# A two-layer block on one Trainium2 core: three of the twelve weight subtractions of each expert go from VectorE to GpSimd

## The reference, cut to what matters

```python
def expert_block(args):
    xb, eb = args                       # rows sent to one of 32 experts
    up = jnp.dot(xb, w_up[eb]) + b_up[eb]            # 1024 -> 2048
    glu, lin = jnp.split(up, 2, axis=-1)
    glu = jnp.minimum(glu, SWIGLU_LIMIT)
    lin = jnp.clip(lin, -SWIGLU_LIMIT, SWIGLU_LIMIT)
    act = glu * jax.nn.sigmoid(SWIGLU_ALPHA * glu) * (lin + 1.0)
    return jnp.dot(act, w_down[eb]) + b_down[eb]     # 1024 -> 1024
```

## Time and profile before

| | us |
|---|---|
| median of 3 runs (lowest and highest) | 2296.3 (2295.66 and 2297.38) |
| the profiled execution, its own time | 2296.3 |
| its span, first to last instruction | 2294.5 |
| PE busy over the span | 2163.4 (94%) |
| DVE busy | 1483.6 (65%) |
| ACT busy | 1200.2 (52%) |
| POOL busy | 74.8 (3%) |

### The profile page before, as it was taken

One profiled execution on the slowest core, in us unless ns is written; L12 is line 12 of the kernel. 1 busy time (PEld: TensorE's weight loads), 2 busy tenths in 40 slices (PEclk: granted clock), 3 DMA queues, 4 the chain that ended last, 5 costly groups with the idle time before them and its releaser, 6 DMA issues. The chain is left out here.

```text
span 2294.5 us, 29210 instructions
## 1 busy us (share of the span) xinstructions
PE 2163.4 (94%) x10208; PEld 1688.1 (74%) x10208; DVE 1483.6 (65%) x1509; ACT 1200.2 (52%) x1252; POOL 74.8 (3%) x51
## 2 busy tenths in 40 slices
PE   7899996899999999999999999999996889799988
PEld 4675345688888888888888888888884478667777
DVE  1303303789999899899898999989995145234401
ACT  1111402677776777777777777777773126522210
POOL 0000000000000000000000000000000013311000
PEclk8998997799999999999999999999998999899999
DMA  9753602598888888888988898898894433223420
GB/s 329 194 177 131 231 13 92 173 307 307 303 302 310 307 308 298 305 305 303 313 304 300 306 304 306 306 305 300 305 315 170 156 126 123 98 74 110 143 78 19
DMA packets 252653, 525.24 MB, mean 229 GB/s; under 512 B 27442, under 2 KB 34714, under 8 KB 252474
## 3 DMA queue, kind: packets, MB, share of 16 engines
q1 hardware_dynamic: 240538, 521.40, 65.8%
q10 hardware_dynamic: 12064, 3.15, 0.9%
HBM read 522.88 MB, written 1.06 MB: 228 GB/s over the span
## 5 line engine op out<-in xcount | busy, mean ns | idle before, releaser
L1197 DVE TENSOR_TENSOR low<-ring_low,high 128x2048 fp32r<-128x2048 f32 x384 | 869.8, 2288 | 115.3 <-ACT high L1328 115.3
L1328 ACT ACTIVATE high<-ring_low 128x2048 fp32r<-128x2048 f32 x384 | 727.8, 1912 | 70.0 <-PE ps L1272 56.1
L1272 PE MATMUL ps<-high,xh 128*128 128x512 f32 x1024 | 298.5, 414 | 0.0
L1272 PE MATMUL ps<-high,xl 128*128 128x512 f32 x1024 | 281.2, 397 | 0.0
L1272 PE MATMUL ps<-low,xh 128*128 128x512 f32 x1024 | 281.1, 396 | 0.0
L1272 PEld LDWEIGHTS ps<-low,xh 128*128 128x128 f32 x1024 | 193.0, 188 | 46.5
L1272 PEld LDWEIGHTS ps<-high,xl 128*128 128x128 f32 x1024 | 190.9, 189 | 43.2
L1272 PEld LDWEIGHTS ps<-high,xh 128*128 128x128 f32 x1024 | 186.7, 190 | 40.6 <-issue 0.3
L1337 ACT ACTIVATE sg<-gl 128x512 f32<-128x512 f32 x64 | 40.4, 631 | 252.2 <-DVE gl L1405 252.2
L1272 PE MATMUL ps<-high,ah 128*128 128x512 f32 x512 | 143.1, 401 | 1.8 <-issue 1.8
L1272 PE MATMUL ps<-low,ah 128*128 128x512 f32 x512 | 143.0, 401 | 0.0
(11 more groups left out here) (469 smaller groups left out, 2795.2 us busy)
## 6 DMA issues: line engine op xcount, KB each, us to landing
ring_low<-in_w_up_dram SPq DMA_DIRECT2D x512, 512.0 KB, 5.7
ring_low<-in_w_down_dram SPq DMA_DIRECT2D x128, 1024.0 KB, 6.8
second_ring<-in_w_in_dram SPq DMA_DIRECT2D x11, 2048.0 KB, 8.2
ring_low<-in_w_in_dram SPq DMA_DIRECT2D x10, 2048.0 KB, 8.5
first_ring<-in_w_ada_dram SPq DMA_DIRECT2D x7, 2048.0 KB, 8.7
ring_low<-in_w_ada_dram SPq DMA_DIRECT2D x5, 2048.0 KB, 7.7
first_ring<-in_ada_w_dram SPq DMA_DIRECT2D x4, 2048.0 KB, 8.1
first_ring<-in_w_in_dram SPq DMA_DIRECT2D x3, 2048.0 KB, 20.7
```

Source lines behind the costliest of these rows:

```text
L1197: eng.tensor_tensor(low[:, sl, :], raw[:, sl, :], high[:, sl, :].bitcast(F32), ALU.subtract)\
L1272: mm = pe.matmul(ps[:, bank + c, :], x[:, 2 * kp + q, :], w[:, q * D + c * 512:q * D + (c + 1) * 512], start=(first and i == 0 and q == 0) ...
L1328: act.activation(high[:, sl, :], raw[:, sl, :], ACT.Copy).then_inc(s("w_high"), 1)
```

## The change

Slabs 3, 6 and 10 of every expert are subtracted by POOL, in a loop of its own, and no longer by DVE. Those subtractions count on a semaphore of their own, `w_low_pool`, and whoever waits for `low` (PE ahead of its third group, SP ahead of a load) waits on the semaphore of the engine that does the slab. ACT's `high_part`, the rings, the look-ahead and the order of everything else stay.

```diff
+        POOL_SLABS = (3, 6, 10)
+        DVE_SLABS = tuple(j for j in range(SLABS) if j not in POOL_SLABS)
...
             def wait_low(eng, e, j):
-                eng.wait_ge(s("w_low"), e * SLABS + j + 1)
+                q, r = divmod(j, SLABS)
+                if r in POOL_SLABS:
+                    eng.wait_ge(s("w_low_pool"), (e + q) * len(POOL_SLABS) + POOL_SLABS.index(r) + 1)
+                else:
+                    eng.wait_ge(s("w_low"), (e + q) * len(DVE_SLABS) + DVE_SLABS.index(r) + 1)
...
+            @block.gpsimd
+            def _(pool):
+                with condition(pool):
+                    with pool.Fori(0, NE) as e:
+                        for j in POOL_SLABS:
+                            low_part(pool, e, j, "w_low_pool")
...
-                        if not (last and j + LEAD >= SLABS):
+                        if (j + LEAD) % SLABS not in POOL_SLABS and not (last and j + LEAD >= SLABS):
                             low_part(dve, e, j + LEAD, "w_low")
```

More of the change, by code:

```diff
@@ L994, in two_layers @@
                        "pm_turned pmT_ready gr_ready ye_high ye_low added aT_high aT_low scattered glu_ready sig_ready "
-                       "steps slab_done w_high w_low filled "
+                       "steps slab_done w_high w_low w_low_pool filled "
                        "raw_in0 raw_in1 raw_in2 raw_in3").split()
```

## The result

The changed kernel takes 2423.8 us in the median of 4 runs (2421.8 to 2426.7), the kernel before 2296.4 (4 runs): a ratio of 1.0551, 95% interval 1.0537 to 1.0565. It is 127 us slower; 124 were forecast. The profiled execution's span is 2420.5 us against 2294.5.

What follows compares the result with a forecast made beforehand. PE was taken to pace the loop. Waits of 1.57 + 1.63 + 0.81 = 4.01 us an expert, times 31 experts = 124 us, on 2296.3 give 2420 us; own range 2395 to 2455, chance 0.70.

Steps and rivals of the forecast that it cites:

- The bound: Loop over the experts: PE sets the pace, DVE at 91% is next; at most some 2 us can be gained.
- The price T: POOL's time for one 128x2048 float32 subtraction: 4.56 us, the middle between 4.05 and 5.07.
- the formula 4.01 + 2 (T - 4.56): Loss per expert in us for another T: the first and third holds grow with T, the second does not.
- rounds 2 and 3 (slab 3): POOL's slab 3 holds DVE's slab 4, adds 0 and 1 come late, PE waits 1.47 and 0.10, together 1.57 us.
- turning matmuls (slab 6): POOL's slab 6 gets ahead of DVE's slab 5, adds 2 and 3 come late, PE waits 1.63 us.
- second `turn_act` (slab 10): POOL's slab 10 holds the second swiglu's multiplies on DVE; PE waits 0.81 us to turn the result.
- Who is first at slab 6: POOL asks for slab 6 at 1017.15, DVE for slab 5 at 1017.77: POOL first by 0.6 us.
- The rival in which DVE is first: DVE's slab 5 precedes POOL's slab 6 if T is about 4.0 or less; only the first wait stays; 2329 us, chance 0.12.
- The hold: POOL and two-SBUF-operand DVE instructions exclude each other until about 0.15 us before the first one's end; T - 0.15 = 4.41 us.
- no hold: Rival: DVE's slab 4 starts while POOL runs, all three waits are zero; 2296 us, less at most 2; chance 0.07.
- The count: 31 experts lose 4.01 us each, 124 us; the first is left out, as it starts from another state and is slower already.
- The granted clock: Rival: PE loses its clock in the new gaps; about 2489 us; chance 0.07 for this or something worse, above 2465.

Runs made afterwards that it cites:

- the run with long memsets: Changed kernel, but each POOL slab is an 8-column subtraction, a 3072-column memset of a spare tile and a 2040-column memset; 2296.2 us, ratio 0.9996.
- both runs with memsets: the run with long memsets, and the changed kernel with three times an 8-column subtraction and a 2040-column memset for each POOL slab, 2498.0 us.

## Why the prediction was right, point by point

**The bound.** PE paces the loop, and DVE's relief is worth nothing: confirmed by the run with slab 6 alone, which takes a subtraction of 2.29 us off DVE and leaves the period at 41.26 us.

**The price T.** 4.56 us was the middle between two rows; POOL's undisturbed subtraction takes 4.64 (slab 3 alone: 4607 to 4667 ns), within both bounds. The 4497 ns of the Trainium skill ("GPSIMD Engine Reference", section 3.1) are 3% below what is measured here. With T = 4.64 the formula 4.01 + 2 (T - 4.56) gives 4.17 us an expert; measured are 45.41 - 41.26 = 4.15.

**The three waits.** Laid over the kernel before, matmul by matmul, PE falls back in an expert like this:

| place | forecast us | measured us (medians over 28 experts) |
|---|---|---|
| rounds 2 and 3 (slab 3) | 1.57 | 1.79 |
| turning matmuls (slab 6) | 1.63 | 1.51 |
| first `turn_act` | counted as nothing | 0.06 |
| second `turn_act` (slab 10) | 0.81 | 0.79 |
| sum | 4.01 | 4.15 |

At the first, PE's round 2 starts 1.57 us late where 1.47 was forecast, of which T explains 0.08; and 0.11 comes on top twice, for the first matmul of each round:

```profile
1070.97 0.39 PE L1260 MATMUL ps<-pmT,yh 128*128 128x256 f32 x1 [1.42 <-DVE hT L1405]
...
1071.57 0.38 PE L1260 MATMUL ps<-pmT,yh 128*128 128x256 f32 x1
```

They take 0.39 and 0.38 us and not the 0.28 of the earlier trace rows, and the next starts 0.22 later and not 0.12. I had 0.10 for round 3, as a wait for add 1, and nothing for the restart; that the 0.10 came out is luck, since round 3 starts no later than its place behind round 2, and loses its 0.11 after its first matmul. Since PE comes later to the second, the wait there is shorter by the same; the sum hardly moves, as the adds set the time and not PE.

**Who is first at slab 6.** The forecast was POOL, by 0.6 us. It was by 0.78 (1070.65 against 1071.43). The rival in which DVE is first did not occur here, but its mechanism is right: with the adds moved, DVE is first, and the wait is gone.

**The hold.** It starts with whoever came and lets the other go about 0.14 us ahead of the end, as in the earlier trace rows; what "no hold" would have given, 2296, is the run with long memsets. The Trainium skill ("SBUF — State Buffer", section "Who interferes with whom") says that only a POOL instruction that reads SBUF meets DVE's two-operand ones; both runs with memsets agree, at 2.29 us.

**The count.** I counted 31 experts. The first loses 0.07 us only (43.56 against 43.50), so there are 30 in the loop and a last one: the beginnings of the first and the last expert are 124.8 us further apart. The last one loses 2.4 us up to PE's last scatter matmul and not 4.15, and the stretches ahead of the experts and behind them are 1.3 us shorter together. So 31 x 4.01 comes this close partly by luck: 4.01 is a little low and 31 a little high.

**The rest.** The granted clock stayed at 1.00 in the loop (470 to 1830 us). The loads cost nothing: ACT waited for them 15.2 us in the whole loop, 10.3 before, ahead of PE's need. That DVE's holds would show as longer instructions was so too, but not two things beside it. The maximum was forecast near 4 to 5 us and is 6.12; the prediction's own times for slab 6 (asked for at 1017.77, had at 1021.56) give 6.1. And the idle time before DVE's subtractions rose, from 115.3 to 160.8 us: without slab 3, DVE waits for ACT's high part of slab 4 (3.61 us in the expert above). The list of three places was also one short, as the runs with slab 3 alone and with slabs 3 and 6 showed: PE's wait for `turned_low` ahead of slab 10 has some 0.2 us to spare before. In the changed kernel it costs nothing: there PE's slab 10 begins 0.41 us after DVE's end, and 0.24 is enough.

## What to carry to other kernels

An instruction that leaves DVE for POOL does not stop costing DVE if it reads SBUF there and DVE's other work has two operands in SBUF: here 6.7 us of DVE's work an expert went, and 9.4 us of holds came (2.75, 3.68 and 3.01 us in the rows above). Before moving, look in the trace for a place where both engines already work and compare the same form's durations; then ask of each instruction that can be held what is queued behind it, and how long its reader can wait. If work must be shared so, put what does not need the port (here the adds that read PSUM) ahead of what may be held: that was worth 109 us.

## What the runs showed of the hardware that I had not expected

- The cost is far from additive: 66, nothing that can be told, and 11 us alone, 127 together, as a late DVE loses the next race for the port.
- The hold hits the short instruction hardest. A POOL subtraction of 8 columns, 0.20 us by itself, took 2.09 behind a DVE subtraction. The run with three such for each slab, of which 81 of 288 took over 1 us, was 201 us slower than the kernel before, more than the change itself.
- PE's first matmul of a round takes 0.10 to 0.11 us more in the changed kernel, in both rounds that depend on the adds, and so does the first turning matmul after its wait (0.33 us against 0.22).
